# GpSimd in place of VectorE for the remainders of three norms' squares, with new step orders, in a two-layer hybrid decoder trunk

## The chip, the core and the metric

The kernel runs on one core of one Trainium2 chip. The metric is the time of one execution on the device, in microseconds (us). The kernel before was run three times: the median is 1242.65 us, the runs lie from 1242.56 to 1242.9 us.

Five engines work side by side, each on its own list of instructions in a fixed order: TensorE (PE in the profile, with PEld for its weight loads), VectorE (DVE), ScalarE (ACT), GpSimd (POOL) and SyncE (SP), which issues the transfers between the device's memory (HBM) and the on-chip buffer. An engine that meets a wait on a semaphore stands still until the semaphore has the value, and everything behind it in its list stands too.

## The reference

Two layers of a trunk for 528 tokens (16 learned meta tokens and 512 of the sequence), model width 1024. Cut to what matters:

```
a = rms_norm(h, attn_norm)
proj = a @ w_in                           # 24 units of 128 columns
dq, dk, iq, ik -> rms_norm (dq, dk only), partial_rope
o_a = dsa_attention(...)                  # index scores, top 128 keys, softmax over them
fq, fk -> rms_norm;  o_b = forgetting_attention(...)
o_c = gla_chunked(...);  o_c = rms_norm(o_c) * silu(gg)
h = h + concat(o_a, o_b, o_c) @ w_out
f = rms_norm(h, ffn_norm);  h = h + (silu(gate) * up) @ w_down
```

The norms of this case are the ones over heads of 64 (dk, dq, fq, fk) or 128 columns (o_c): x times the inverse root of the mean of its squares.

## The kernel before

**Data.** Features lie on the 128 partitions, tokens along the row. A weight unit is a 128x1024 tile. Every product of TensorE that must be exact is made of parts: ScalarE rounds a tile to a high part (`whi`, `xhi`), another engine subtracts it from the tile to get the low part (`wlo`, `xlo`), and TensorE sums high times high, high times low and low times high. So each weight unit of the projections needs a rounding on ScalarE (L1713) and a split on GpSimd (L891, four instructions of 128x256) before TensorE can do its low pass (L1136).

**The norm of a head unit k.** ScalarE squares the unit twice: in full into `sqb` (L1784) and rounded into `sq_parts[:, 1]` (L1785). One subtraction, the remainder, fills `sq_parts[:, 0]`. TensorE sums both parts over the head with a matrix of ones (`norm`, L1150, four matmuls). ScalarE makes the inverse root with a logarithm and an exponential (L1758, L1793), VectorE multiplies the unit by it (L2276). There is one `sqb` and one `sq_parts`, so ScalarE squares the next unit only after TensorE's sums of the one before. Eleven units are normed in each layer, in the order of NORM_ORDER: 0 (dk with ik), 4 and 5 (dq), 6 and 7 (fq), 8 and 9 (fk), and 16 to 19 (o_c). For the first three the remainder is on VectorE (`square_left`, L2285, semaphore `sq_left`), for the other eight on GpSimd (`square_parts`, L984, semaphore `sq_split`).

**From norm 0 to the index scores.** After norm 0, SyncE gathers the rotary rows of units 0, 1 and 2 into `xnb` (L826, three transfers), TensorE swaps them (`rope`, L1159), VectorE rotates them (L2303 to L2306), SyncE spreads them back (L836), ScalarE and VectorE split keys (`split_k`, L1798 and L2312, tile `kk`) and queries (`split_q`, L1809 and L2319), and TensorE makes the index products (`index`, L1204), which ScalarE reads (L1904) and VectorE sums.

**Order.** In the mixers (projections and attention, ahead of the feed-forward part) the order of the steps on each engine is a string of letters for each layer and engine (STEPS_OF, L261), one letter for each chain of steps; the chains are listed in L184. BANKS_OF (L285) gives the PSUM bank of each small job of TensorE. Of a projection half there are three pieces: two of high products (L1130, L1131) and one low pass (L1136). Behind the mixers everything is written out in the code.

Of the kernel before, what the change touches and what calls it, by code (L numbers as in the profile page):

```python
# [260 lines left out]
STEPS_OF = (  # L261
    {PE: "AAAAAAAAAAAABAAAAADAAAAAAFAAALAAAAAAAAAADAAAMMADAMMMMMMAMAAAMADAAAAPAAAADAAAAAAAAAPXXAAAAADXAXAAAAaL"
         "bAALAADAAAAAAAAXXXAXXdAXaXAYAYXXMMAAAbMAAMaAAdYZXAZXAYAXAYZZbXAAYAAAAZYYdXZZALXAAPARRAPLAYXZXYMAMaAb"
         "aALYdZAAYZXAXXAAYAZZbAYYZXXdZXZLYAAXYTSSZaRAATRbTARSSATTYAaAAdDXAZZYYXXXDZZbYAYAAdZDAYZAaAADZYAXXZbA"
         "XYAAXdAXYZaYXYZXZYXZbYYaZZYdZZfbfdfff",
     ACTE: "AABCDAAPIHLIACHADCIMMIDMMMMMMACMMDCIIAADCJOPAPIIPJDXAXXCXaALJLDAJAXXXXeaXXYYXMMMAXMaeYXXAYYPXXAKYYeX"
           "YLXPAPLXYYMXMaaYLAYeXXXXYYYeXLYYTaXAATTXXTTCYaUeCDXYYCXDYXAeYDXCYDYaUXXUYXXeAYaYUXXYYXXVYVVYVYAaee",
     DVEE: "AAACADAAAFAPIAAHIACHADCMMIIDMMMMMMAAFADANNNAADNINAINAXAIIANNXXOXDANANNNANNNDNANNNcXAXXXXPeXXAAXMMXMM"
           "NANNcAPPXXPNAXANcPeXAAXeNNXNNRRANNXMMAMXMAcNNNXNNeAXXANcNXXeNXNXASSRRNcNRSSNNANNAUeXNDXXNNcDXNAeADNN"
           "NNDXXUAXcXAAeXXUUXVVXcVWVWWWcee",  # L270
     POOLE: "QAAAQAAACACAACAACAQQAAAAQQAAAAACCCCAAA",
     DMAE: "AAEEEGAAAAEEGAAAAAAAAAAAAAAAAAA"},
    {PE: "AAAAAAAAABADAAAAAAFAAAAAALAMMDAAMADAMMMMAMMAAMADAAAADAAAAAAAAXXADAAAAYXAXYAMaMAMAADMAAAALLAAPXZZAYAP"
         "AAAAAYXXAAAXAAAAYYZZAAXbaAAYAAXAALZAYYZXZXAZAAAYXAMaAAAARARAALMAPPALbLASSTARATRSTdSRATYZZXYTAAYZYXZd"
         "XXbDAAYYZZadADXZZYXXbXXYAaZZYYXDAAdZZYYXbXYZXZZYaYXdZbXYZdXYZaXYZXYZXYbYDZZdYZaZbfdffff",
     ACTE: "BACADAAIIHACLIMMDHACMIDMMMMCMMAADCODMAIICADIIXXCXYYXMMAaMMADJJJPJLLAPPAXPYYXXAYYAXAaXLYYXYPXYXAMKaAL"
           "MPPXLALTTTAeTYYUTCXAYYXeDCXXYaeYUDYXXXYCaAYYUDXXXCeYYUYXXYaXeYYXeXVVaYAXYVXYXYXDYYVaee",
     DVEE: "AACDAAAFIIAAHCIMMDAHCMIDMMAMMFNAMDNAADIINXAAADXIIXXAMMMOMNNNNADNANPNANXNNNANNNNAPAXXANNNNXNNNAXPAXcA"
           "NPPAXXMNAPMNMXANARRNNMAANNNSNNSRNNRASNcRNSeNXNNNNXXecXADNNeUNXAXXDcXNNXXNNDNUAXcXXeUUVXecXVeXWVXXXcW"
           "DVWWcee",  # L280
     POOLE: "QQAAAAAACACAACACAAQQAAQAAAQAAAACCCAACA",
     DMAE: "AEEEAAGAAEEAGAAAAAAAAAAAAAAAAAA"},
)

BANKS_OF = (  # L285
    "0022023023012323220023103300030130213012013000232021011203210220202013200230321030210213013031030102"
    "0201203212002132030121203020203023013020320312",
    "0202012203203032000123210203102021030201231302300312030202020202031102010311303132031011203103013122"
    "0320132020220310130130101302301203",
)  # L290
# [2751 lines left out]
```

## Time and profile before

One profiled execution took 1242.44 us; its span, from the first to the last instruction, is 1240.7 us, so that 1.74 us lie around it. It is 0.21 us below the median of the three runs.

| what | before |
|---|---|
| median of 3 runs | 1242.65 us |
| profiled execution | 1242.44 us, span 1240.7 us |
| granted clock of TensorE | 1.0 over the span |
| TensorE busy | 1233.1 us, 99% of the span |
| VectorE, ScalarE, GpSimd busy | 83%, 57%, 16% |
| remainders on VectorE, on GpSimd | 6 and 16 |

The mixers of layer 0 lie between about 20 and 248 us of the span, those of layer 1 between about 647 and 865 us. A row of a timeline has the start, the time, the engine, the line of the kernel, what is written and read, and in brackets how long the engine was idle before it and what ended that. Matmuls are pipelined, so their times overlap; the distance from one start to the next tells how fast they go.

### The profile page before, as it was taken

The page shows a single profiled execution, that of the slowest core. Times are in us where ns is not written, and L with a number is a line of the kernel's source. Part 1 is how long each engine was busy: PE and PEld are TensorE (multiplying, and loading weights), DVE is VectorE, ACT ScalarE, POOL GpSimd, SP SyncE. Part 2 cuts the span into 40 slices and gives each one's busy share as a digit, 9 for nine tenths or more (in the row PEclk, how much of TensorE's full clock was granted, in tenths as well). Part 3 has the DMA queues.
Part 4 walks back from the last instruction along what each step waited for, and adds up shares of the span by engine and source line. Part 5 has one row for each costly group of instructions (what it writes and reads, how often), then busy time and mean ns, then how long its engine had stood idle before and what let it go on. Part 6 is the DMA issues. An engine that isn't in the chain of part 4 may idle for free.

```text
span 1240.7 us, 23938 instructions
## 1 busy us (share of the span) xinstructions
PE 1233.1 (99%) x9379; PEld 1185.1 (96%) x9379; DVE 1028.2 (83%) x1700; ACT 701.4 (57%) x1165; POOL 201.5 (16%) x264
## 2 busy tenths in 40 slices
PE   9999999999999999999999999999999999999999
PEld 9999999999999999999998999888889999998998
DVE  5788979588999999897666888985899999989765
ACT  6684547665555555753355765495665555558332
POOL 3565322100000000000035664230000000000000
PEclk9999999999999999999999999999999999999999
DMA  5222110132322221233323222110323322212333
GB/s 215 87 74 82 55 52 18 36 136 100 105 103 103 102 102 69 86 103 116 107 86 109 89 72 83 35 35 18 136 102 126 113 104 102 102 69 85 120 119 119
DMA packets 27244, 114.02 MB, mean 92 GB/s; under 512 B 3456, under 2 KB 3968, under 8 KB 21760
## 3 DMA queue, kind: packets, MB, share of 16 engines
q1 hardware_dynamic: 26704, 111.74, 26.6%
q8 instruction: 73, 1.20, 0.4%
q10 hardware_dynamic: 432, 0.80, 0.2%
q14 instruction: 35, 0.29, 0.1%
HBM read 108.79 MB, written 2.10 MB: 89 GB/s over the span
## 4 chain that ended last, share of the span: by engine, by line
PE 98%; ACT 1%; DVE 0%; issue 0%; POOL 0%; ACTq 0%; DVEq 0%
PE ps L1415 23%; PE ps L1421 11%; PE ps L1027 11%; PE ps L1130 7%; PE ps L1136 7%; PE ps L1131 7%; PE ps L1033 5%; PE ps L1499 5%; PE ps L1535 4%; PE ps L1256 3%; PE ps L1504 2%; PE ps L1540 2%; PE ps L1204 2%; PE ps L1229 2%; PE ps L1239 1%; PE ps L1150 1%
## 5 line engine op out<-in xcount | busy, mean ns | idle before, releaser
L891 POOL TENSOR_TENSOR wlo<-raw,whi 128x256 fp32r<-128x256 f32 x192 | 150.5, 816 | 144.7 <-ACT whi L1713 144.2
L1130 PE MATMUL ps<-xhi,whi 128*128 128x264 f32 (+1 forms) x616 | 172.1, 308 | 0.0
L1131 PE MATMUL ps<-xlo,whi 128*128 128x264 f32 (+1 forms) x616 | 167.3, 300 | 0.0
L1130 PEld LDWEIGHTS ps<-xhi,whi 128*128 128x128 f32 x616 | 116.1, 188 | 4.2 <-issue 0.4
L1131 PEld LDWEIGHTS ps<-xlo,whi 128*128 128x128 f32 x616 | 116.2, 189 | 3.4
L1713 ACT ACTIVATE whi<-raw 128x1024 fp32r<-128x1024 f32 x74 | 78.0, 1055 | 60.7 <-PE ps L1033 28.2
L1136 PE MATMUL ps<-xhi,wlo 128*128 128x264 f32 (+1 forms) x616 | 99.8, 304 | 0.0
L1136 PEld LDWEIGHTS ps<-xhi,wlo 128*128 128x128 f32 x616 | 85.2, 188 | 4.0
L1415 PE MATMUL ps<-fhi,hi_a 128*128 128x264 f32 (+1 forms) x352 | 88.2, 283 | 0.0
L1415 PE MATMUL ps<-flo,hi_a 128*128 128x264 f32 (+1 forms) x352 | 88.1, 282 | 0.0
L1415 PE MATMUL ps<-fhi,hi_b 128*128 128x264 f32 (+1 forms) x320 | 80.3, 283 | 1.8 <-ACT s L2037 1.8
L1415 PE MATMUL ps<-flo,hi_b 128*128 128x264 f32 (+1 forms) x320 | 80.3, 283 | 0.0
L2037 ACT ACTIVATE w_part<-ps 128x264 f32<-128x264 f32 (+1 forms) x42 | 16.3, 388 | 97.4 <-PE ps L1421 97.4
L923 POOL MEMSET lr_parts<- 80x532 f32 x2 | 1.1, 544 | 414.8 <-DVE wlo L2756 400.6
L2148 ACT ACTIVATE whi<-raw 128x1024 fp32r<-128x1024 f32 (+2 forms) x42 | 38.3, 913 | 50.4 <-PE ps L1504 30.4
L1415 PE MATMUL ps<-xlo,hi_a 128*128 128x264 f32 (+1 forms) x264 | 66.5, 283 | 0.0
L1415 PE MATMUL ps<-xhi,hi_a 128*128 128x264 f32 (+1 forms) x264 | 66.3, 283 | 0.0
L1415 PEld LDWEIGHTS ps<-flo,hi_a 128*128 128x128 f32 x352 | 66.3, 188 | 0.0
L1415 PEld LDWEIGHTS ps<-fhi,hi_a 128*128 128x128 f32 x352 | 66.2, 188 | 0.0
L1415 PEld LDWEIGHTS ps<-fhi,hi_b 128*128 128x128 f32 x320 | 60.3, 188 | 2.1 <-ACT hi_a L1996 2.1
L1415 PEld LDWEIGHTS ps<-flo,hi_b 128*128 128x128 f32 x320 | 60.3, 188 | 0.0
L1415 PE MATMUL ps<-xlo,hi_b 128*128 128x264 f32 (+1 forms) x240 | 59.9, 282 | 0.0
(377 smaller groups left out, 3885.1 us busy)
## 6 DMA issues: line engine op xcount, KB each, us to landing
raw<-in_weights SPq DMA_DIRECT2D x115, 512.0 KB, 3.5
raw<-in_groups SPq DMA_DIRECT2D x42, 1024.0 KB, 4.8
h<-in_hT SPq DMA_DIRECT2D x7, 264.0 KB, 6.4
out_hT<-h SPq DMA_DIRECT2D x7, 256.0 KB, 4.6
cst<-in_consts SPq DMA_DIRECT2D x1, 908.5 KB, 8.7
xnb<-feat SPq DMA_DIRECT2D x10, 66.5 KB, 2.1
feat<-xnb SPq DMA_DIRECT2D x10, 66.5 KB, 2.1
cst<-in_consts SPq DMA_DIRECT2D x1, 532.0 KB, 3.5
```

The lines of the kernel that those rows point to most:

```text
L891: ins = nc.gpsimd.tensor_tensor(wlo[:, b, of], raw[:, b, of], whi[:, b, of].bitcast(F32), ALU.subtract)
L1027: nc.tensor.matmul(bank(bank_no, cut.stop - cut.start), whi[:, b, k % KT], x(k)[t][:, cut], start=(first and k == ks[0] and t == 0), stop= ...
L1033: ins = nc.tensor.matmul(bank(bank_no, cut.stop - cut.start), wlo[:, b, k % KT], x(k)[0][:, cut], start=False, stop=(last and k == ks[-1]))
L1130: nc.tensor.matmul(o, whi[:, k % 2, n], xhi[:, n, cut], start=(n == 0), stop=False)
L1131: nc.tensor.matmul(o, whi[:, k % 2, n], xlo[:, n, cut], start=False, stop=False)
L1136: ins = nc.tensor.matmul(o, wlo[:, k % 2, n], xhi[:, n, cut], start=False, stop=(n == KT - 1))
L1415: nc.tensor.matmul(bank(bank_no, width), high[:, of], x(i)[t], start=(begins and i == 0 and t == 0), stop=False, skip_group_check=True)
L1421: ins = nc.tensor.matmul(bank(bank_no, width), low, x, start=False, stop=(n == PAIRS - 1), skip_group_check=True)
L1499: nc.tensor.matmul(to, whi[:, slot, k], hidden_tiles(k0 + k)[t][:, cut], start=(begins and k == 0 and t == 0), stop=False, skip_group_chec ...
L1535: nc.tensor.matmul(down_bank(l, bank_no), high(i), x(i)[t], start=(begins and i == 0 and t == 0), stop=False, skip_group_check=True)
L1713: return nc.scalar.activation(whi[:, b], raw[:, b], ACT.Copy).then_inc(hi_done, 1)
L2148: nc.scalar.activation(whi[:, slot, 0:tiles], raw[:, slot, 0:tiles], ACT.Copy).then_inc(hi_done, 1)
```

## The change

The remainders of units 0, 4 and 5 go to GpSimd as well: the two kinds of step become one (`square`), the semaphore `sq_left` goes, and TensorE waits for `sq_split` alone. The strings of STEPS_OF and BANKS_OF are replaced as a whole, for both layers and all engines.

```diff
-LEFT_TO_VECTOR = (DKIK, DQ, DQ + 1)
-LEFT_TO_GPSIMD = (FQ, FQ + 1, FK, FK + 1, GV, GV + 1, GV + 2, GV + 3)
...
-def square_step(k):
-    return ("square_left" if k in LEFT_TO_VECTOR else "square_parts", k)
...
-        "square": [square_step(k) for k in NORM_ORDER],
+        "square": [("square", k) for k in NORM_ORDER],
...
-     POOLE: "QAAAQAAACACAACAACAQQAAAAQQAAAAACCCCAAA",
+     POOLE: "QAACQAAACACCAACAACAACQQAAAAQQAAAAACCCCAAA",
...
-    "prenorm": (PE, ACTE), "square_left": (ACTE, DVEE), "square_parts": (ACTE, POOLE), "norm": (PE, ACTE, DVEE),
+    "prenorm": (PE, ACTE), "square": (ACTE, POOLE), "norm": (PE, ACTE, DVEE),
...
-        self.sq_left = sem(f"sq_left_of{l}")
...
-                    if k in LEFT_TO_VECTOR:
-                        pe.wait_ge(ev.sq_left, LEFT_TO_VECTOR.index(k) + 1)
-                    else:
-                        pe.wait_ge(ev.sq_split, LEFT_TO_GPSIMD.index(k) + 1)
+                    pe.wait_ge(ev.sq_split, SQUARES[k] + 1)
...
-                def square(k):
-                    dve.wait_ge(ev.sq_ready, 2 * SQUARES[k] + 2)
-                    nc.vector.tensor_tensor(sq_parts[:, 0], sqb[:, 0], sq_parts[:, 1].bitcast(F32), ALU.subtract).then_inc(ev.sq_left, 1)
```

Three places show what the new strings move. The lines of the changed kernel have other numbers (the remainder is L976 there, the weight split L883, the sums of a norm L1139, the low pass L1128, the rounding of a unit L1702).

TensorE, layer 0, around the sums of norm 0; before:

```order
L1131 MATMUL ps<-xlo,whi 128x264
L1130 MATMUL ps<-xhi,whi 128x264
L1131 MATMUL ps<-xlo,whi 128x264
L1150 MATMUL ps<-sq_parts,ones_r 128x266 x4
L1136 MATMUL ps<-xhi,wlo 128x264 x8
L1130 MATMUL ps<-xhi,whi 128x264
```

and changed:

```order
L1123 MATMUL ps<-xlo,whi 128x264
L1122 MATMUL ps<-xhi,whi 128x264
L1123 MATMUL ps<-xlo,whi 128x264
L1128 MATMUL ps<-xhi,wlo 128x264 x8
L1139 MATMUL ps<-sq_parts,ones_r 128x266 x4
L1122 MATMUL ps<-xhi,whi 128x264
```

The sums of norm 0 stand one low pass later. The `rope` products stand as many projection pieces from the start as before, so that one piece less lies between the two.

GpSimd, layer 1, from the clearing of `q_odd` to the weight splits; before:

```order
L946 MEMSET k_fox 64x2x532 x2
L947 MEMSET q_odd 64x1064
L910 COPY q_odd<-cst 4x532 x2
L891 TENSOR_TENSOR wlo<-raw,whi 128x256 x24
L984 TENSOR_TENSOR sq_parts<-sqb,sq_parts 128x532
```

and changed:

```order
L938 MEMSET k_fox 64x2x532 x2
L939 MEMSET q_odd 64x1064
L902 COPY q_odd<-cst 4x532 x2
L976 TENSOR_TENSOR sq_parts<-sqb,sq_parts 128x532
L883 TENSOR_TENSOR wlo<-raw,whi 128x256 x16
L976 TENSOR_TENSOR sq_parts<-sqb,sq_parts 128x532
L883 TENSOR_TENSOR wlo<-raw,whi 128x256 x4
```

The remainder of unit 0 stands ahead of every weight split of the layer, and that of unit 4 ahead of the fifth.

ScalarE, layer 0, from the first query part to the rounding behind the squares of unit 4; before:

```order
L1809 ACTIVATE q_split<-feat 64x528
L1798 ACTIVATE kk<-feat 64x528 x2
L1818 ACTIVATE v_dsa<-ps 128x4x64
L1820 ACTIVATE v_meta<-ps 16x64 x4
L1821 ACTIVATE w_idx<-ps 128x20
L1809 ACTIVATE q_split<-feat 64x528
L1713 ACTIVATE whi<-raw 128x1024
L1784 ACTIVATE sqb<-feat 128x532
L1785 ACTIVATE sq_parts<-feat 128x532
L1798 ACTIVATE kk<-feat 64x528 x2
L1713 ACTIVATE whi<-raw 128x1024
```

and changed:

```order
L1798 ACTIVATE q_split<-feat 64x528 x2
L1787 ACTIVATE kk<-feat 64x528 x2
L1702 ACTIVATE whi<-raw 128x1024
L1807 ACTIVATE v_dsa<-ps 128x4x64
L1809 ACTIVATE v_meta<-ps 16x64 x4
L1810 ACTIVATE w_idx<-ps 128x20
L1787 ACTIVATE kk<-feat 64x528 x2
L1773 ACTIVATE sqb<-feat 128x532
L1774 ACTIVATE sq_parts<-feat 128x532
L1702 ACTIVATE whi<-raw 128x1024
```

The second half of the key split (`kk`) now stands ahead of the squares of unit 4.

## Rows read from the trace of the kernel before

**Rows 1.** The page: busy time by engine; chain that ended last, by engine.
```profile
PE 1233.1 (99%) x9379; PEld 1185.1 (96%) x9379; DVE 1028.2 (83%) x1700; ACT 701.4 (57%) x1165; POOL 201.5 (16%) x264
...
PE 98%; ACT 1%; DVE 0%; issue 0%; POOL 0%; ACTq 0%; DVEq 0%
```
**Rows 2.** Waits of TensorE, whole span: who for whom, us, times, longest.
```profile
PE ps L1415 <- ACT s L2037: 1.8, 2, 0.9
PE ps L1004 <- DVE kk L2216: 1.2, 1, 1.2
PE ps L1204 <- ACT relu L1904: 0.5, 1, 0.5
PE ps L1204 <- DVE q_keys L2319: 0.3, 1, 0.3
PE ps L1192 <- issue: 0.2, 1, 0.2
PE ps L1150 <- POOL sq_parts L984: 0.2, 1, 0.2
PE ps L1204 <- DVE mix_hi L2319: 0.2, 1, 0.2
```
**Rows 3.** The remainders by source line: ns min/median/max, first and last start.
```profile
L984 POOL TENSOR_TENSOR sq_parts<-sqb,sq_parts x16: 1320/1339/1807, 60.4 to 829.6; 128x532 fp32r<-128x532 f32 x16
...
L2285 DVE TENSOR_TENSOR sq_parts<-sqb,sq_parts x6: 711/868/1139, 25.2 to 675.2; 128x532 fp32r<-128x532 f32 x6
```
**Rows 4.** Timeline of GpSimd, then ScalarE, layer 0, 19 to 26 us.
```profile
19.73 5.60 POOL L891 TENSOR_TENSOR wlo<-raw,whi 128x256 fp32r<-128x256 f32 x8 [1.01 <-ACT whi L1713]
...
24.53 0.64 ACT L1785 ACTIVATE sq_parts<-feat 128x532 fp32r<-128x532 f32 x1
```
**Rows 5.** TensorE from norm 0: chain of waits (start, us, what), then timeline.
```profile
26.78 0.98 PE ps L1136 x8
...
32.51 1.11 PE L1159 MATMUL ps<-xnb,cst 96*96 96x266 f32 x4
```
**Rows 6.** SyncE's gather before `rope`: timeline, then `xnb` transfers' landing times.
```profile
29.03 1.82 SPq L826 DMA_DIRECT2D xnb<-feat  x3
...
DMA to landing us min/median/max: 1.9/2.1/3.4
```
**Rows 7.** Timeline of ScalarE, layer 0, the squares of units 4 and 5.
```profile
44.52 0.63 ACT L1785 ACTIVATE sq_parts<-feat 128x532 fp32r<-128x532 f32 x1
45.06 1.29 ACT L1798 ACTIVATE kk<-feat 64x528 fp32r<-64x528 f32 x2
...
47.82 0.69 ACT L1758 ACTIVATE rnb<-ps,cst 128x532 f32<-128x532 f32 x1
...
49.63 0.63 ACT L1785 ACTIVATE sq_parts<-feat 128x532 fp32r<-128x532 f32 x1
```
**Rows 8.** Timeline of TensorE, layer 0, norms 4, 5, 6 and three index waits.
```profile
46.65 0.65 PE L1150 MATMUL ps<-sq_parts,ones_r 128*128 128x266 f32 x4
...
51.67 0.74 PE L1150 MATMUL ps<-sq_parts,ones_r 128*128 128x266 f32 x4
...
53.58 0.42 PE L1204 MATMUL ps<-kk,mix_hi 128*128 128x144 f32 x2 [0.19 <-DVE mix_hi L2319]
54.32 0.42 PE L1204 MATMUL ps<-kk,q_keys 128*128 128x144 f32 x2 [0.32 <-DVE q_keys L2319]
...
57.21 0.64 PE L1204 MATMUL ps<-kk,q_split 128*128 128x400 f32 x2 [0.45 <-ACT relu L1904]
...
61.95 0.68 PE L1150 MATMUL ps<-sq_parts,ones_r 128*128 128x266 f32 x4
```
**Rows 9.** Timeline of ScalarE, layer 0, the squares of unit 6.
```profile
59.69 0.64 ACT L1785 ACTIVATE sq_parts<-feat 128x532 fp32r<-128x532 f32 x1
...
61.16 0.50 ACT L1904 ACTIVATE relu<-ps 128x400 f32<-128x400 f32 x1 [0.44 <-PE ps L1204]
```
**Rows 10.** Timeline of layer 1's start: GpSimd, then TensorE.
```profile
645.95 1.30 POOL L910 COPY q_odd<-cst 4x532 f32<-4x532 f32 x2
647.33 3.22 POOL L891 TENSOR_TENSOR wlo<-raw,whi 128x256 fp32r<-128x256 f32 x4
...
648.50 0.66 PE L1150 MATMUL ps<-sq_parts,ones_r 128*128 128x266 f32 x4
...
650.83 2.02 PE L1136 MATMUL ps<-xhi,wlo 128*128 128x512 f32 x8
```
**Rows 11.** Weight splits of GpSimd, ns min/median/max: whole span, then 44 to 53 us.
```profile
L891 POOL TENSOR_TENSOR wlo<-raw,whi x192: 720/738/1773, 19.7 to 845.6; 128x256 fp32r<-128x256 f32 x192
...
L891 POOL TENSOR_TENSOR wlo<-raw,whi x8: 734/1147/1216, 44.2 to 50.9; 128x256 fp32r<-128x256 f32 x8
```

More of the change, by code:

```diff
@@ L261 @@
 STEPS_OF = (
[L262 to L270, printed above, removed]
-     POOLE: "QAAAQAAACACAACAACAQQAAAAQQAAAAACCCCAAA",
-     DMAE: "AAEEEGAAAAEEGAAAAAAAAAAAAAAAAAA"},
@@ L273 @@
[L273 to L282, printed above, removed]
+    {PE: "AAAAAAAAAAAABAAAAAADAAAAAFAAAAAALAAAAAAAADAAMMADAMMMMAMMAMMAAADAPAAAAAAAAAAADAXXAAAAAPAXAAADAAAXAALA"
+         "AALAAADaAAbAAAAXXAAXXXdXAXaAbXYAMMYAXAMAAMAadXZYYAAZAZZbYAXXXAAAYAAZdYAAYXXAAZALPARRAZPLAXYYXZMAMaAA"
+         "AbaAZdZLYAYXXZZYbAAXXYAAYZdAXXYZLXZYTSSRAaAATRZTbRSSATTYAZadAAZDXXAYYXAYDZZXbAAYDZAdAAAYYZDaAZAAXZbX"
+         "XAYXAAdYXZaXYYZXYZXZbYYaZZYdZZbfdffff",
+     ACTE: "AABCDAAPIIHALHCAIDCIMMDMMMMMMMMCADIAPCIOADIICAXPAJXPDCAXXLJLAaJDJXXXAXXaeYXXMMXYAMMaYXYYXXAPYXAeYeKX"
+           "XYALPXPLYYMMXaaXeLYYAXXYAXXeYYYLYXTXaTXTTATYCeaUDCXXYYDYCAXXDCeYYYaUDUXXYXXeYAXaYUXYXYXVYVVaYYVAee",
+     DVEE: "AAAADAAFAAAPIIAHHAADMMIIDMMMMMMAAFNADANANIIAADANXNNXIINAAXONNNDXAAANNNPANNDNNNXXNcXAAXXXAXXMeMMMXNNc"
+           "APNPAXAPXXNcNAAXPeeAXXNNNARRNNXMNMMXMAAcNNNeXXNNNXXcAAeXXNXNSSRNNNRcRSSNNNAAeNNXDXXANDUXcNNDAeNNAANN"
+           "DXUXXXceXUAAXXUVXVcVVWWWWcee",
+     POOLE: "QAACQAAACACCAACAACAACQQAAAAQQAAAAACCCCAAA",
+     DMAE: "AAEEEGAAAEEGAAAAAAAAAAAAAAAAAAA"},
@@ new lines @@
+    {PE: "AAAAAAAAABADAAAAAAFAAAAAALMMADAAMADAMMMAMAAAMMDMAAAAADAAAAAADXAAXYAAAXXAAMMYAAMAAaADAMZZALAAALAXYPAA"
+         "AAYPYAXAXZAAAXZbYAAAYXAAAZaAAXAAAZZLAAYYXAXZYAAAAMAXAAaRRAAALMAPPAALLASTASRATRbSTdSRZZAYTYXZZTYXbYXA"
+         "dXDAZAdaYYZAZZXDAXXbYAXYYXZZaAYDXAZZYYXbdXYZXZaYZYXZdbXYZdXYZaXZYXYZXYbYDZYdaZZZbffdfff",
+     ACTE: "BACDAAAIIHAICLMMDHCMAIDMMAMMCAMDCJOAIDCIMMADXIIPXCXYMMMYXAaAJJDJLMALXYPAYPPXXXYAAAaYYLXXYYYPXXMKAaLM"
+           "PPAXLLTTATUeYAYTXTCYYeCXDXYaeAYUDXCYXXXYUXYaYDXXAYYUXYXeaYAYXeXYeXCYaXVVYYXXYXDYaVYVee",
+     DVEE: "AADAAFAAIIAHIMMDAHMIDMMAMMFAMDNNAADIIAAXDIXIAXXMNMMMAPOAANNNDNNNNANNXNNNNNAANNXXNAAXNNNNcAAXPPAXNNAP"
+           "PXXMMPMXNAARRANNNMNAANNNSNNSRNNRSAcSReUNNXNNNXXNcXeNADNNeXNNXXDAcNXXNNXDANUUXcXUXVeVVXceXeXXXXcWWDVW"
+           "Wcee",
+     POOLE: "QQCAAAACACAACACCAACAAQQQAAAAAQAAAACCCACAA",
+     DMAE: "AEEEAAGAAEAEGAAAAAAAAAAAAAAAAAA"},
@@ L283 @@
 )
 BANKS_OF = (
[L286 to L289, printed above, removed]
+    "0022023023012323220230013000330130210301302100230211201220312020202102300232031032021031031031031002"
+    "0201203212010233020211302020203203103020320312",
+    "0202012203203030202013212301002020312030121230300312003202020202013102010313130130213013012010133201"
@@ L290 @@
+    "2302320120202310130130101302302103",
 )
 ON = {
-    "prenorm": (PE, ACTE), "square_left": (ACTE, DVEE), "square_parts": (ACTE, POOLE), "norm": (PE, ACTE, DVEE),
+    "prenorm": (PE, ACTE), "square": (ACTE, POOLE), "norm": (PE, ACTE, DVEE),
     "gather": (DMAE,), "rope": (PE, DVEE), "spread": (DMAE,), "split_k": (ACTE, DVEE),
@@ L985, in square @@
                     halved[0] += 1
-                do = dict(proj=proj, square_parts=square, masks=masks, clear_fox=clear_fox, spread_sums=spread_sums, clear_even=clear_even,
+                do = dict(proj=proj, square=square, masks=masks, clear_fox=clear_fox, spread_sums=spread_sums, clear_even=clear_even,
                           clear_gla_even=clear_gla_even, clear_gla_odd=clear_gla_odd)
@@ L1969, in gla_mix @@
                     nc.scalar.activation(mix_hi[:, 4 + hd], feat[:, place(GG + hd)], ACT.Copy).then_inc(ev.gla_hi, 1)
-                do = dict(prenorm=prenorm, proj=proj, square_left=square, square_parts=square, norm=norm, split_k=split_k, split_q=split_q_hi, part=part, even_q=even_q,
+                do = dict(prenorm=prenorm, proj=proj, square=square, norm=norm, split_k=split_k, split_q=split_q_hi, part=part, even_q=even_q,
                           turn_tile=turn_tile,
@@ L2532, in gla_lo @@
                                             ALU.subtract).then_inc(ev.gla_split, 1)
-                do = dict(proj=proj, square_left=square, norm=norm, rope=rope, split_k=split_k, split_q=split_q_lo, gate_split=gate_split, gate_log=gate_log, gate_sum=gate_sum, gate_arg=gate_arg,
+                do = dict(proj=proj, norm=norm, rope=rope, split_k=split_k, split_q=split_q_lo, gate_split=gate_split, gate_log=gate_log, gate_sum=gate_sum, gate_arg=gate_arg,
                           fox_log=fox_log, decays=decays, index=index, topk=topk, lowest=lowest,
```

## The prediction

> **What bounds the kernel.** Three views were read. First the busy times and the chain that ended last: TensorE is busy for 1233.1 us of a span of 1240.7, and the chain is 98% TensorE [rows 1]. The change takes no instruction from TensorE and adds none; its matmuls come in another order. So what counts is where TensorE stands still. The second view, its waits over the whole span, says how little that is: seven kinds, 4.4 us together, of which the two waits of 1.8 and 1.2 us lie outside the mixers. That leaves 1.4 us in the mixers, five kinds of 0.2 to 0.5 us [rows 2], and only there do the new strings reach. Of the engines that the change touches, only 0.2 of it waits for GpSimd and none for a remainder on VectorE: its line L2285 is not among those waited for [rows 2]. The third view, timelines around the moved steps, tells how much time each had to spare.
>
> So the removal as such is worth next to nothing, and the question is what GpSimd and the new orders make late.
>
> **What the removal frees.** Six remainders (three units, two layers) leave VectorE: six times a median of 0.87 is 5.2 us [rows 3], at 83% busy [rows 1]. TensorE waits for VectorE in the mixers for 0.3 + 0.2 us [rows 2]. These are the most that a freer VectorE can give.
>
> **What it adds.** Six remainders of the same 128x532 on GpSimd, at a median of 1.34 us there (1.32 to 1.81) [rows 3]. GpSimd is busy for 16% [rows 1], so 8 us more are nothing as a total. What costs is the place: a remainder stands in GpSimd's list between weight splits, waits there for ScalarE's squares, and TensorE's sums wait for it; 1.34 against 0.87 also lengthens each of the six chains by about 0.5 us.
>
> **Layer 0, norm 0 and the rope.** GpSimd's first eight splits end at 19.73 + 5.60 = 25.33, the squares at 24.53 + 0.64 = 25.17 [rows 4], so the remainder runs from 25.33 to 26.67. TensorE has norm 0 one low pass later; the low pass that now comes ahead of it takes 0.98 and began at 26.78 behind norm 0 [rows 5]. With 0.65 for four sums of a norm [rows 8], norm 0 began at about 26.1 and will at about 27.1: later than 26.67, no wait. But the rope keeps its place in the count of projection pieces, at 32.51 [rows 5], and its chain starts 0.98 later. Before, the three gathers end at 29.03 + 1.82 = 30.85; the third is issued at about 30.3 and lands 2.1 later by the median, at 32.4 [rows 6]. The rope had 0.1 us to spare or a little more, and now lacks 0.8 to 1.0. I take +0.9.
>
> **Norm 4.** On ScalarE the second pair of key halves goes ahead of the squares: the time to square is 45.15, when the squares of unit 4 end now (44.52 + 0.63), so two squares of 0.63 or a little more reach 45.15 + 1.29 = 46.4 if the pair is only put ahead, and up to 47.3 if they are also released 0.9 later by the late rope [rows 7]. The remainder ends at 47.8 to 48.7, with 1.81 for it at 49.2. TensorE had norm 4 at 46.65 [rows 8]; it comes one piece later (0.97, as the low pass of [rows 5]) and 0.9 of the rope's wait later, at 48.5. Between nothing and 0.7; I take +0.4, near the later squares, since keys wait for the rope as well.
>
> **Norm 5.** It needs norm 4 first, as there is one `sq_parts`. From the logarithm of norm 4 (47.82) to the end of the squares of unit 5 (49.63 + 0.63) ScalarE takes 2.44 [rows 7]. Norm 4 at 48.9 and its 0.65 [rows 8] make 49.6; plus 2.44 is 52.0, plus 1.34 is 53.4, at worst 53.8. TensorE's place for norm 5 is 51.67 [rows 8] plus the 1.3 lost so far, 53.0. I take +0.6 of 0.4 to 0.9.
>
> **Index and norm 6.** Behind two such waits the index products come later than their parts, and the three small waits of 0.19, 0.32 and 0.45 [rows 8] go: −1.0. The squares of unit 6, which end at 60.3, now stand behind the two relus of 400 keys, the first of which begins at 61.16 [rows 9]; norm 6 was at 61.95 [rows 8]. Two relus of 0.50, two squares of 0.64 and 1.34 would reach past it by more than 1 us if TensorE had not itself moved back by 1 to 2 us and a piece. Between 0 and 1.4; I take +0.4, nearer to none, as TensorE's delay is the nearest row. Layer 0: 0.9 + 0.4 + 0.6 − 1.0 + 0.4 = +1.3.
>
> **Layer 1, the first weight unit.** GpSimd's list now has the remainder of unit 0 ahead of all splits. It is free at 645.95 + 1.30 = 647.25; the remainder takes the place of the split at 647.33 and ends at 648.67. Norm 0 stood at 648.50: +0.2. The first unit's four splits took 3.22, to 650.55, and the low pass that needs them started at 650.83 [rows 10], 0.28 behind. Now they end at 651.9, or at 651.6 if each takes the median of 0.74 [rows 11]: the low pass is late by 0.8 to 1.1 in all. I take +1.0, the 0.2 of norm 0 in it. Queued behind these splits are all later ones, but those had units of lead to spare.
>
> **The rest of layer 1.** One block of index products stands ahead of a projection piece that it used to follow, so its key parts may be late: 0 to 0.6, taken as +0.2. The wait of 0.2 for `sq_parts` of GpSimd and the 0.2 of no seen releaser [rows 2] belong to a norm and a gate that now come one piece later: −0.4. Layer 1: +0.8. Other moved steps are costed at nothing, because TensorE stands for 0 us at their like in the list of waits [rows 2]; with that cover gone each costs its chain's excess, a few tenths.
>
> **Sum.** +1.3 + 0.8 = +2.1 on the profiled execution of 1242.44 (span 1240.7 and 1.74 around it) is 1244.5 us. The median of the runs is 0.21 higher, which I leave in the range.
>
> **A rule that speaks for more.** Between 44 and 53 us the eight splits took a median of 1.15 us against 0.74 over the whole span, so GpSimd is slowed there by something [rows 11]. The Trainium skill, "SBUF — State Buffer", section "Who interferes with whom", says that a VectorE instruction with two inputs in that buffer contends with a GpSimd instruction that reads it, and that whichever issues first holds the shared ports for the whole instruction. By that rule a remainder can cost 1.34 plus a VectorE operation of 0.7, about 2.05 (an estimate with that page's rule), against the longest seen, 1.81; the trace agrees in kind, and the sum would be 1247 instead of 1244.5 if all six were hit, which is in the second case's upper part.
>
> **The rivals.** *GpSimd's queue becomes the bound (slower).* A remainder that waits for squares holds every split behind it, and those hold low passes. Six remainders at 1.81 instead of 1.34 are +2.8 at most if all lie on the path, and norm 6 at its end of 1.4 is +1.0 more than taken. For it: the splits at 1.15 us where norms 4 and 5 lie [rows 11], and the 0.28 us of spare at the first low pass of layer 1 [rows 10]. Against it: GpSimd's 16%, and that a wait at one step covers the next. About half of these, +1.8 on my sum, is 1246.3; up to 1248. It decides from new waits of 3.9 us, which less the 1.4 of old ones pass 2.5 us.
>
> *Nothing new waits.* The late parts are covered because TensorE's order gives each norm a piece more, and only old waits go, or the new cost equals them: −1.4 to +0.5, 1241.0 to 1243.0, with 1241.9 as its time. For it: norms 0 and 4 do stand a piece later. Against it: the rope does not, and its slack of 0.1 is in the rows [rows 5, 6]; the first split of layer 1 is delayed by a whole remainder and no row shows time for it [rows 10].
>
> *Faster by more than the measure.* What can be told from no change is about 0.2%, 2.5 us, here below 1240.2. All mixer waits of TensorE are 1.4 [rows 2], so this needs matmuls that themselves go faster in the new order. No row shows such.
>
> **How the numbers follow.** Forecast 0.48, with its own range of 1243.2 to 1245.1; queue as the bound 0.35; nothing new 0.12; faster 0.05. The first and third lie within 2.5 us of 1242.65: same 0.60. Slower 0.35, faster 0.05. The range from 1242.3 (half of the third case left out) to 1247.2 (the tail of the second left out) leaves about 2 in 10.
>
> **What would show it.** In the waits of TensorE after: at the rope, for the `xnb` transfers, about 0.9; at the norms for `sq_parts` of GpSimd, 1 to 1.6 together; at the low pass of layer 1, for `wlo` of GpSimd, about 0.8 to 1; and the three index waits gone. The 4.4 us of waits become about 6.5. VectorE's busy time falls by 5 us and GpSimd's rises by 8. I am wrong if the waits in the mixers sum to less than 1.4 us, if they pass 5, or if the span moves and they do not; in the last case the order itself would change how fast matmuls follow each other.

## The result: slower by 4.8 us, above the forecast range

The changed kernel takes 1247.43 us in the median (1246.87 to 1247.91, 6 runs) against 1242.61 (6 runs) for the kernel before: a ratio of 1.0038, with a 95% interval of 1.0028 to 1.0048. The forecast was 1244.5, its range 1242.3 to 1247.2: the sign was right, the size less than half of what was measured. The profiled execution took 1246.87 us, 0.56 below the median, with a span of 1245.1.

The page of the changed kernel, busy times by engine and the chain that ended last [rows 1]:

```profile
PE 1234.4 (99%) x9379; PEld 1185.2 (95%) x9379; DVE 1021.6 (82%) x1694; ACT 702.6 (56%) x1165; POOL 206.6 (17%) x270
...
PE 93%; POOL 2%; DVE 2%; ACT 2%; issue 1%; DMA 1%; SPq 0%; ACTq 0%; DVEq 0%; POOLq 0%
```

VectorE is freed of 6.6 us and GpSimd has 5.1 more, where 5 and 8 were forecast; GpSimd's remainders add 7.9, its weight splits take 3.2 less. The chain now leaves TensorE for 7% of the span instead of 2%: it runs mostly through GpSimd, VectorE and ScalarE. The waits of TensorE (engine, tile and line, then whom for: us, times, longest) [rows 2]:

```profile
PE ps L1139 <- POOL sq_parts L976: 2.4, 4, 0.9
PE ps L1404 <- ACT s L2026: 1.8, 2, 0.9
PE ps L996 <- DVE kk L2205: 1.2, 1, 1.2
PE ps L1148 <- DMA xnb<-feat: 0.8, 1, 0.8
PE ps L1128 <- POOL wlo L883: 0.6, 2, 0.4
```

All five small waits of the mixers are gone and 3.8 us of new ones have come, 3.0 of them for GpSimd. So the list holds 6.8 us where it held 4.4, and shows only 2.4 of the 4.4 us by which the span grew. The rest stands in no listed wait: TensorE's idle time (span less busy time) grew by 3.1 us in all, short gaps included, and its busy time by 1.3. The new waits in TensorE's timeline (start, us, line, operation; in brackets the idle time and its end):

```profile
33.68 0.44 PE L1148 MATMUL ps<-xnb,cst 96*96 96x266 f32 x1 [0.78 <-DMA xnb<-feat]
...
54.04 0.36 PE L1139 MATMUL ps<-sq_parts,ones_r 128*128 128x266 f32 x1 [0.89 <-POOL sq_parts L976]
...
63.97 0.36 PE L1139 MATMUL ps<-sq_parts,ones_r 128*128 128x266 f32 x1 [0.60 <-POOL sq_parts L976]
...
75.05 0.39 PE L1128 MATMUL ps<-xhi,wlo 128*128 128x264 f32 x1 [0.20 <-POOL wlo L883]
...
680.05 0.36 PE L1139 MATMUL ps<-sq_parts,ones_r 128*128 128x266 f32 x1 [0.32 <-POOL sq_parts L976]
...
703.82 0.36 PE L1139 MATMUL ps<-sq_parts,ones_r 128*128 128x266 f32 x1 [0.61 <-POOL sq_parts L976]
707.48 0.39 PE L1128 MATMUL ps<-xhi,wlo 128*128 128x264 f32 x1 [0.44 <-POOL wlo L883]
```

These are the rope, norms 5 and 6 and the low pass of unit 9 in layer 0, then norms 5 and 8 and the low pass of unit 10 in layer 1. Units 6 and 8 had their remainder on GpSimd before as well, and with the new orders alone (below) their norms still wait, 0.49 and 0.31 us; so these waits come at least in part from the order of the lists.

To see what each layer lost, three marks were read in every trace: the first projection product of layer 0's mixers, and the first product of the feed-forward part of each layer. Before:

```profile
20.94 0.48 PE L1130 MATMUL ps<-xhi,whi 128*128 128x264 f32 x1
...
294.93 0.28 PE L1415 MATMUL ps<-xhi,hi_a 128*128 128x264 f32 x1
...
909.81 0.28 PE L1415 MATMUL ps<-xhi,hi_a 128*128 128x256 f32 x1
```

and after the change:

```profile
21.14 0.48 PE L1122 MATMUL ps<-xhi,whi 128*128 128x264 f32 x1
...
297.47 0.28 PE L1404 MATMUL ps<-xhi,hi_a 128*128 128x264 f32 x1
...
914.22 0.28 PE L1404 MATMUL ps<-xhi,hi_a 128*128 128x256 f32 x1
```

From mark to mark layer 0 costs 2.34 us more (276.33 against 273.99) and layer 1 costs 1.87 more; from the last mark to the end the traces differ by 0.01. The first mark varies by up to 0.5 us from the kernel before's although nothing ahead of it was changed; the marks leave that part out. They come from one execution of each kernel, and executions of one kernel differ by up to 2.2 us (1243.54 to 1245.74 for orders_norm0_back), so single tenths of them prove nothing.

### The profile page after: what moved, and what is told of

Its sections match the earlier page's. It is cut to its first block, busy times and chain, and to the rows that moved or that the text cites. A ratio compares the mean times of both kernels' runs of the same rounds, so it can differ in the third digit from the quotient of the medians.

```text
span 1245.1 us, 23934 instructions
## 1 busy us (share of the span) xinstructions
PE 1234.4 (99%) x9379; PEld 1185.2 (95%) x9379; DVE 1021.6 (82%) x1694; ACT 702.6 (56%) x1165; POOL 206.6 (17%) x270
## 4 chain that ended last, share of the span: by engine, by line
PE 93%; POOL 2%; DVE 2%; ACT 2%; issue 1%; DMA 1%; SPq 0%; ACTq 0%; DVEq 0%; POOLq 0%
PE ps L1404 23%; PE ps L1410 11%; PE ps L1019 10%; PE ps L1128 6%; PE ps L1122 6%; PE ps L1123 5%; PE ps L1025 5%; PE ps L1524 4%; PE ps L1488 4%; PE ps L1245 3%; PE ps L1529 2%; PE ps L1493 2%; PE ps L1218 2%; PE ps L1193 1%; PE ps L1228 1%; POOL wlo L883 1%
## 5 line engine op out<-in xcount | busy, mean ns | idle before, releaser
L883 POOL TENSOR_TENSOR wlo<-raw,whi 128x256 fp32r<-128x256 f32 x192 | 147.3, 799 | 146.7 <-ACT whi L1702 146.3
L1702 ACT ACTIVATE whi<-raw 128x1024 fp32r<-128x1024 f32 x74 | 78.1, 1055 | 59.4 <-PE ps L1025 29.9
L1128 PE MATMUL ps<-xhi,wlo 128*128 128x264 f32 (+1 forms) x616 | 100.2, 305 | 0.7 <-POOL wlo L883 0.6
L1128 PEld LDWEIGHTS ps<-xhi,wlo 128*128 128x128 f32 x616 | 84.6, 188 | 5.5 <-POOL wlo L883 1.6
L1404 PE MATMUL ps<-xhi,hi_b 128*128 128x264 f32 (+1 forms) x240 | 59.9, 282 | 0.0
```

The source lines that it names most:

```text
L883: ins = nc.gpsimd.tensor_tensor(wlo[:, b, of], raw[:, b, of], whi[:, b, of].bitcast(F32), ALU.subtract)
L1128: ins = nc.tensor.matmul(o, wlo[:, k % 2, n], xhi[:, n, cut], start=False, stop=(n == KT - 1))
L1404: nc.tensor.matmul(bank(bank_no, width), high[:, of], x(i)[t], start=(begins and i == 0 and t == 0), stop=False, skip_group_check=True)
L1702: return nc.scalar.activation(whi[:, b], raw[:, b], ACT.Copy).then_inc(hi_done, 1)
```

## The experiments

At first there were two theories. O: the new orders cost the time (rope, norms 6 and 8 wait although their remainders did not move). Q: the remainder on GpSimd costs it, longer by 0.5 us and in a queue with the weight splits. Times are medians; "before" is the kernel before in the same comparison; the last two columns are the differences from mark to mark against the trace before.

| kernel | us | before | ratio (95%) | layer 0 | layer 1 |
|---|---|---|---|---|---|
| changed | 1247.43 | 1242.61 | 1.0038 (1.0028 to 1.0048) | +2.34 | +1.87 |
| engine_alone | 1246.68 | 1242.9 | 1.0032 (1.0020 to 1.0044) | +2.83 | +1.36 |
| orders_alone | 1245.9 | 1242.9 | 1.0023 (1.0014 to 1.0032) | +2.92 | +0.49 |
| double_remainders | 1254.76 | 1242.9 | 1.0097 (1.0081 to 1.0112) | +6.21 | +5.48 |
| mended | 1247.57 | 1242.9 | 1.0038 (1.0025 to 1.0052) | +3.32 | +1.76 |
| unit0_moved | 1243.97 | 1242.52 | 1.0013 (1.0004 to 1.0022) | +0.64 | +0.85 |
| unit4_moved | 1244.92 | 1242.52 | 1.0018 (1.0009 to 1.0027) | +1.56 | +0.96 |
| unit5_moved | 1244.48 | 1242.52 | 1.0016 (1.0007 to 1.0025) | +1.07 | +0.49 |
| before_mended | 1242.98 | 1242.52 | 1.0004 (0.9995 to 1.0013) | +0.01 | −0.05 |
| unit5_held | 1246.9 | 1242.4 | 1.0034 (1.0021 to 1.0048) | +3.03 | +1.33 |
| before_held | 1245.53 | 1242.4 | 1.0025 (1.0015 to 1.0034) | +2.64 | +0.62 |
| orders_norm0_back | 1244.82 | 1242.47 | 1.0018 (1.0009 to 1.0027) | +1.08 | +0.33 |
| after_norm0_back | 1247.07 | 1242.47 | 1.0036 (1.0022 to 1.0050) | +2.60 | +2.17 |

**The engine alone.** The changed code with all lists of before; only GpSimd's got the six remainders, as the squares come ready.

```diff
-     POOLE: "QAAAQAAACACAACAACAQQ...        (layer 0)
+     POOLE: "QAACAQACACACACAACAACAQQ...
-     POOLE: "QQAAAAAACACAACACAAQQ...        (layer 1)
+     POOLE: "QQCAAAACACACACAACACAAQQ...
```

> The six remainders on GpSimd, all other orders as before (GpSimd's own list takes each where its squares are ready). Theory O (the new orders cost most of the 4.8 us): at most +1.8 us over before, worked out as 0.6 at norm 0 of layer 0 (remainder 25.33 to 26.67 against TensorE at 26.07), 0.6 at the start of layer 1, 0.4 at norm 5 of layer 1: 1243.0 to 1244.4. Theory Q (the remainder on GpSimd, longer and in a queue, costs most): +3 or more, 1245.6 and up, with waits of TensorE for sq_parts of GpSimd at norms 4 and 5.

**The orders alone.** The new lists of the change, with the three remainders back in VectorE's list and out of GpSimd's.

```diff
-     DVEE: "AAAADAAFAAAPIIAHHAADMMIID...     (layer 0)
+     DVEE: "AAACADAAFAAAPIIAHHACADCMMIID...
-     DVEE: "AADAAFAAIIAHIMMDAHMID...         (layer 1)
+     DVEE: "AACDAAFAAIIAHICMMDAHCMID...
```

> The orders of the changed kernel, the six remainders back on VectorE. Theory O: the wait at the rope (0.8), those at norm 6 of layer 0 and norm 8 of layer 1 (0.6 each, both of units whose remainder was always on GpSimd) and at a low pass (0.4) stay: 1245.3 to 1247. Theory Q: these go with the queue, at most +1.5 us over before, up to 1244.1.

Measured: +3.8 us for the engine alone, +3.0 for the orders alone, +4.8 for both. Neither theory holds by itself: each half alone costs more than the theory that lays the loss on the other half allows (+1.8 and +1.5). The marks separate them by layer. In layer 1 the halves add up (1.36 and 0.49 against 1.87), and the engine is nearly three quarters of it. In layer 0 they do not (2.83 and 2.92 against 2.34): there the orders take back part of what the engine costs, and the engine part of the orders'. With the lists of before, the split of unit 6 and the remainder of unit 4 meet in GpSimd's list; this is its timeline in the kernel with the engine alone, and what TensorE then waits for:

```profile
46.22 1.34 POOL L976 TENSOR_TENSOR sq_parts<-sqb,sq_parts 128x532 fp32r<-128x532 f32 x1 [4.99 <-ACT sq_parts L1774]
47.51 4.22 POOL L883 TENSOR_TENSOR wlo<-raw,whi 128x256 fp32r<-128x256 f32 x4
```

```profile
51.78 0.39 PE L1128 MATMUL ps<-xhi,wlo 128*128 128x264 f32 x1 [1.41 <-POOL wlo L883]
```

GpSimd stands for 4.99 us in front of a remainder whose squares are not made yet, and behind it the split, which began at 44.2 in the kernel before [rows 11], starts at 47.51. With the remainder on VectorE the two ran side by side. The changed kernel puts the split first and norm 4 one piece later, and has no 1.41 there.

**Twice the remainder.** The changed kernel with a second instruction behind each of the six.

```diff
+ if SQUARES[k] < 3:
+     nc.gpsimd.tensor_tensor(sq_parts[:, 0], sqb[:, 0], ..., ALU.subtract).then_inc(ev.sq_first, 1)
+     pool.wait_ge(ev.sq_first, SQUARES[k] + 1)
+     nc.gpsimd.tensor_tensor(sq_parts[:, 0], ..., ALU.add).then_inc(ev.sq_split, 1)      (sq_parts[:, 0] added to itself)
```

> The changed kernel with a second GpSimd instruction of 128x532 behind each of the six remainders (it adds the low part to itself, so the low part of these squares is doubled). Each extra takes about 1.4 us. Theory Q: norms 4 and 5 of both layers and the first low pass of layer 1 stand directly behind the remainder, +1.4 at five of six places: +5 to +7 over the changed kernel, about 1253. Theory O: the orders have room at most places, +1 to +4: 1248.4 to 1251.4, and less than 1.4 per place.

The second instruction and who waited for it, by source line:

```profile
L980 POOL TENSOR_TENSOR sq_parts<-sq_parts x6: 1071/1072/1176, 27.0 to 686.4; 128x532 fp32r<-128x532 f32 x6
...
  PE ps L1145: 8.2, 6
```

Six times 1.07 is 6.4 us; the kernel became 7.0 us slower (11.86 over the kernel before, against 4.82 for the changed kernel). TensorE waited for all six. So next to nothing covers a longer remainder in these places (in the changed kernel the sums begin 0.47 us behind it at norm 0 of layer 0, 0.14 to 0.20 us at the other five), and theory Q has this much right: on GpSimd, each sits on the path. No run doubles a remainder on VectorE.

**One unit at a time.** The lists of before, with one unit's remainder moved to GpSimd in both layers. Here the theories are P (the price depends on what stands beside it) and E (each costs alike).

```diff
-LEFT_TO_VECTOR = (DKIK, DQ, DQ + 1)
+LEFT_TO_VECTOR = (DKIK, DQ)                 (for unit 5; the others likewise)
-     POOLE: "QAAAQAAACACA...                 (layer 0)
+     POOLE: "QAACAQAAACACA...  (unit 0)   "QAAAQACAACACA...  (unit 4)   "QAAAQAACACACA...  (unit 5)
```

> The kernel before with only unit 0's remainder on GpSimd (both layers), all other orders as before. Theory P (a remainder costs by what stands beside it in GpSimd's list): norm 0 of layer 0 +0.6, start of layer 1 +0.6, so +1.2 us over before. Theory E (any remainder on GpSimd costs alike, a third of the +3.8 that all three units cost): +1.3. This run tells them apart only with the next two.

> The kernel before with only unit 4's remainder on GpSimd, placed ahead of the split of unit 6. Theory P: in layer 0 the split waits for the squares at 45.15 and its low pass comes late by 1.4 to 1.6, nothing in layer 1: +1.5 us over before. Theory E: +1.3, in both layers alike.

> The kernel before with only unit 5's remainder on GpSimd, placed ahead of the split of unit 7, which has 8 us to spare in layer 0. Theory P: nothing in layer 0, 0.4 to 0.6 at norm 5 of layer 1: +0.3 to +0.8 us over before. Theory E: +1.3.

Measured: +1.45, +2.4 and +1.96 us. The intervals reach about 1.1 us to either side, so the times alone do not tell the units apart and do not exclude E; nor do they tell whether such prices add up (the three make 5.8 us, all three at once cost 3.8 with the engine alone). By the marks P is right on unit 0 (0.64 and 0.85), on unit 4 in layer 0 (1.56) and on unit 5 in layer 1 (0.49). It is wrong at two places: unit 4 in layer 1 (0.96 where nothing was expected) and unit 5 in layer 0 (1.07 where nothing was). Both have the same main cause. With unit 5 moved, TensorE in layer 0 waits like this:

```profile
54.31 0.42 PE L1204 MATMUL ps<-kk,mix_hi 128*128 128x144 f32 x2 [0.29 <-DVE mix_hi L2319]
55.47 0.42 PE L1204 MATMUL ps<-kk,q_keys 128*128 128x144 f32 x2 [0.74 <-DVE q_keys L2319]
...
58.72 0.45 PE L1204 MATMUL ps<-kk,q_split 128*128 128x400 f32 x1 [0.81 <-ACT relu L1904]
```

It waits for VectorE, which has one instruction less to do. The two instructions by source line, before and with unit 5 moved (ns min/median/max):

```profile
L2319 DVE TENSOR_TENSOR mix_hi<-feat,mix_hi x1: 702/702/702, 52.7 to 52.7; 64x528 fp32r<-64x528 f32 x1
L2319 DVE TENSOR_TENSOR q_keys<-feat,q_keys x1: 704/704/704, 53.5 to 53.5; 64x528 fp32r<-64x528 f32 x1
```

```profile
L2319 DVE TENSOR_TENSOR mix_hi<-feat,mix_hi x1: 1121/1121/1121, 53.0 to 53.0; 64x528 fp32r<-64x528 f32 x1
L2319 DVE TENSOR_TENSOR q_keys<-feat,q_keys x1: 1127/1127/1127, 54.2 to 54.2; 64x528 fp32r<-64x528 f32 x1
```

and GpSimd at the same time, with unit 5 moved:

```profile
50.82 1.34 POOL L984 TENSOR_TENSOR sq_parts<-sqb,sq_parts 128x532 fp32r<-128x532 f32 x1 [2.41 <-ACT sq_parts L1785]
52.11 3.80 POOL L891 TENSOR_TENSOR wlo<-raw,whi 128x256 fp32r<-128x256 f32 x4
```

The split of unit 7 ended at 52.1 before the move. Behind the remainder it runs until 55.9, beside VectorE's key and query parts, and both slow down: VectorE's from 0.70 to 1.12, the splits to 0.95 each. In layer 1, unit 4's move does the same to VectorE's remainder of unit 5 (1.13 instead of 0.76) and to the scaling and the key parts ahead of it, and norm 5 waits 0.86 for it. The Trainium skill, "SBUF — State Buffer", section "Who interferes with whom", has the rule (a VectorE instruction with two inputs in that buffer and a GpSimd instruction that reads it contend); the traces agree, with 0.70 against 1.12.

**Holding the split away.** To test this (theory C: the split beside VectorE's chain costs the time; D: the longer remainder does), the split of unit 7 waits until VectorE has scaled unit 5, in both layers, once with unit 5 moved, once in the kernel before.

```diff
  def proj(k, hf, p):
+     if k == 5:
+         pool.wait_ge(ev.normed, 3)
```

> The kernel with only unit 5's remainder on GpSimd, and GpSimd's split of unit 7 held until VectorE has scaled unit 5 (it waits for that semaphore; its low pass has over 1 us to spare after that). With the remainder ahead of it, that split lay beside VectorE's mix_hi, q_keys and scaling, which took 1.12 to 1.13 us instead of 0.70 to 0.77. Theory C (the moved split slows VectorE's chain of two-input instructions): they take 0.70 to 0.78 again, the 1.1 us lost in layer 0 shrink to 0.2 to 0.4, time 1243.4 to 1243.8. Theory D (the longer remainder alone delays the chain): layer 0 keeps its 1.1 us, time 1244.2 to 1244.8.

> The kernel before with the same hold on the split of unit 7, all remainders on VectorE. Theory C: VectorE's scaling of unit 4 and the remainder of unit 5, at 1.15 and 1.12 us beside that split, take 0.7 to 0.9; the index products' waits of 0.19 and 0.32 shrink or go: 0.2 to 0.6 us less than before. Theory D: as before within 0.2.

Both times are far outside what either theory expected, +4.5 and +3.1 us. The part that was to be tested came out as C says: with unit 5 moved and the split held, VectorE takes

```profile
L2321 DVE TENSOR_TENSOR mix_hi<-feat,mix_hi x1: 702/702/702, 51.9 to 51.9; 64x528 fp32r<-64x528 f32 x1
L2321 DVE TENSOR_TENSOR q_keys<-feat,q_keys x1: 705/705/705, 52.6 to 52.6; 64x528 fp32r<-64x528 f32 x1
```

and the index waits of 0.29 and 0.74 shrink to less than 0.1. TensorE gains by it up to there. These are the first mark and the `q_keys` products in the kernel before with the split held:

```profile
20.55 0.48 PE L1132 MATMUL ps<-xhi,whi 128*128 128x264 f32 x1
...
53.03 0.42 PE L1206 MATMUL ps<-kk,q_keys 128*128 128x144 f32 x2
```

They lie 32.48 us apart, against 33.38 in the kernel before [rows 8], 0.9 less; with unit 5 moved the hold gains 1.2 (32.86 against 34.06).

But the split has to be somewhere: now it lies beside the sums of the scores, which also read two tiles. Two of 128x144 take 1.70 there instead of 0.77 with unit 5 moved and the split not held. ScalarE waits for these sums to free its `relu` buffers, TensorE for ScalarE, 2.5 us in one piece. This is VectorE with unit 5 moved, not held:

```profile
56.52 0.77 DVE L2400 SCALAR_TENSOR_TENSOR score<-relu,w_idx,score 128x144 f32<-128x144 f32 x2
```

This is VectorE, unit 5 moved and held:

```profile
54.55 1.70 DVE L2402 SCALAR_TENSOR_TENSOR score<-relu,w_idx,score 128x144 f32<-128x144 f32 x2
56.28 0.71 DVE L2407 SCALAR_TENSOR_TENSOR score<-score,causal 128x144 f32<-128x144 f32 x1
```

and these are ScalarE, in the second of its two waits for VectorE, and TensorE:

```profile
57.97 0.94 ACT L1906 ACTIVATE relu<-ps 128x272 f32<-128x272 f32 x2 [1.23 <-DVE score L2398]
...
58.42 0.79 PE L1206 MATMUL ps<-kk,q_split 128*128 128x400 f32 x2 [2.52 <-ACT relu L1906]
```

So the slowing that C speaks of is shown, in both directions; the shorter time that it forecast is not. The same 3 us of GpSimd's work cost TensorE 0.9 us where they lay in the kernel before (beside the scaling of unit 4 and the remainder of unit 5), 1.2 beside the key and query parts, and a wait of 2.5 us in place of 0.45 beside the sums. In the kernel before with the hold, a gain of 0.9, this longer wait (+2.0), the slower clock behind it (+1.3, last section) and 0.6 in layer 1 make 3.0 of the 3.1 us.

**Pieces moved ahead of what waits.** In the changed kernel, and then in the kernel before.

```diff
  mended (layer 0, TensorE): a piece ahead of the rope and of norm 4, two ahead of norms 5 and 6
-  ...AAAAADAAAAAFA...   ...DAAMMADAMMMMAMMAMMAAADAPA...
+  ...AAAAADAAAAAAF...   ...ADAMMAAADMMMMMMAMMAAAAADP...
  before_mended (layer 0, TensorE):
-  ...DAMMMMMMAMAAA...
+  ...DAAMMMMMMAMAA...
```

> The changed kernel with projection pieces moved ahead of the steps that wait in its trace: one ahead of the rope, one ahead of norm 4, two ahead of norm 5, two ahead of norm 6 in layer 0; one ahead of norms 5 and 8 in layer 1, and GpSimd's split of unit 10 ahead of the remainder of unit 8 there. The remainders stay on GpSimd. Theory O: the waits of 0.78, 0.89, 0.60 and of 0.32, 0.61, 0.44 go, 2.5 to 3.6 us less: 1243.8 to 1245. Theory Q: the waits only move to the next step, at most 1 us less: 1246.4 and up.

> The kernel before with one projection piece moved ahead of the index products that wait 0.19 and 0.32, one ahead of those that wait 0.45 (layer 0), and one ahead of norm 7 of layer 1 (0.20). If TensorE waits there for want of a piece in front: 0.7 to 1.1 us less than before. If the wait moves on to the next product of the same chain, as in the changed kernel with pieces moved: within 0.4 us of before, with new waits behind the old places.

Mended, the changed kernel loses its norm waits but for 0.2 us and takes the same time: 1247.57 against 1247.43. TensorE waits one step further on:

```profile
55.73 0.31 PE L1193 MATMUL ps<-kk,mix_hi 128*128 128x144 f32 x1 [0.50 <-DVE mix_hi L2304]
56.47 0.31 PE L1193 MATMUL ps<-kk,q_keys 128*128 128x144 f32 x1 [0.32 <-DVE q_keys L2304]
59.76 0.45 PE L1193 MATMUL ps<-kk,q_split 128*128 128x400 f32 x1 [0.86 <-ACT relu L1893]
67.13 0.39 PE L1181 MATMUL ps<-lr_parts,w_parts 80*128 80x266 f32 x1 [0.85 <-ACT rnb L1747]
```

The kernel before does it too: its 0.19 and 0.32 go, and norm 6, which had no wait, gets 0.73 (for `sq_parts` of GpSimd, at 61.80). In layer 1 the wait of 0.20 at norm 7 goes, and norm 8, which had none, gets 0.41 (at 701.62). The sum is zero. So in these stretches the chain over ScalarE, VectorE and GpSimd is about as long as TensorE's work, and a wait that is pushed off comes back further down.

**Norm 0 one piece earlier.** As it stood before, once with VectorE's remainders and once with GpSimd's.

```diff
-    {PE: "AAAAAAAAAAAABAAAAAADAAAAAF...
+    {PE: "AAAAAAAAAAAABAAAAADAAAAAAF...
```

> The new orders with VectorE's remainders, and norm 0 of layer 0 one projection piece earlier, where it stood in the kernel before. VectorE's remainder is done there before TensorE comes, so nothing waits at norm 0 and the rope's wait of 0.77 goes. If that wait is a loss of its own: 0.6 to 1.0 us less than with the new orders alone, 1244.9 to 1245.3. If what it gave back is waited for again at norms 4, 5 and 6, which hang on the same chain of keys: under 0.4 us less, 1245.5 and up.

> The changed kernel with norm 0 of layer 0 one piece earlier. GpSimd's remainder ends at 26.82 there and TensorE comes at 26.3: a new wait of about 0.5 for it, and the rope's 0.78 falls to 0.3 or less. If both are losses of their own: 0 to 0.4 us less than the changed kernel, 1247.0 to 1247.4; if the chain behind the rope takes it up, the same within 0.2, or up to 0.5 more.

With VectorE's remainder the rope's wait goes, and the loss falls from 3.0 to 2.35 us over the kernel before; the interval (1.0009 to 1.0027) overlaps that of the orders alone, so the size is open. Layer 0's marks fall from 2.92 to 1.08, but its profiled execution was its fastest (1243.54). With GpSimd's remainder the gain against the changed kernel is 0.2 us by the two differences to the kernel before, which is less than can be told, since the wait at norm 0 takes its place:

```profile
26.64 0.36 PE L1139 MATMUL ps<-sq_parts,ones_r 128*128 128x266 f32 x1 [0.55 <-POOL sq_parts L976]
...
49.06 0.36 PE L1139 MATMUL ps<-sq_parts,ones_r 128*128 128x266 f32 x1 [0.64 <-POOL sq_parts L976]
```

The rope has no wait here, norm 4 gets 0.64 where the changed kernel had none listed (its remainder took 1.90 us here, see below). With GpSimd's remainder, which ends later, either place of norm 0 costs about the same; with VectorE's the old place is the better one. No version was faster than the kernel before.

## Why the prediction was right or wrong

Measured is the difference of each step's start to the next step's start in the two traces.

| term | predicted | measured |
|---|---|---|
| rope | +0.9 | +0.9 |
| norm 4 | +0.4 | +0.2 |
| norm 5 | +0.6 | +0.9 |
| three index waits | −1.0 | −1.3 |
| norm 6 | +0.4 | +0.7 |
| all else in layer 0 | 0 | +0.9 |
| first unit of layer 1 | +1.0 | +0.6 |
| index block of layer 1 | +0.2 | +0.2 |
| two old waits of layer 1 | −0.4 | −0.7 |
| all else in layer 1 | 0 | +1.8 |
| ahead of the mixers | 0 | +0.2 |
| sum on the profiled execution | +2.1 | +4.4 |

**What was right.** No run shows a gain from VectorE's freed time, and the waits at the rope (0.78 for 0.9), norm 5 and norm 6 stand where they were put. The index waits went, as said. The list of waits came out as forecast in its sum, 6.8 us for 6.5, though not in its parts (2.4 for the remainders where 1 to 1.6 were said, nothing listed at the first low pass of layer 1); but it does not hold all that was lost. The first unit of layer 1 was taken too dear: its four splits took 2.83 us in place of 3.22 [rows 10].

**What failed** is one step: "Other moved steps are costed at nothing, because TensorE stands for 0 us at their like in the list of waits [rows 2]; with that cover gone each costs its chain's excess, a few tenths." The end of the sentence names the loss, but the sum has it at 0. These steps cost 2.7 us, more than the whole gap of 2.3. In layer 1 these are norm 8 with 0.77, the low pass of unit 10 behind it with 0.70, norm 5 with 0.39 and norm 6 with 0.29, less 0.4 elsewhere; in layer 0 the low pass of unit 9 with 0.5 and, for the rest, small changes around the steps that moved. A list of waits says where nothing was lost, not how much there was to spare. Norm 8 of layer 1 is not on the list of the kernel before, and these are its remainder and its sums there:

```profile
700.28 1.33 POOL L984 TENSOR_TENSOR sq_parts<-sqb,sq_parts 128x532 fp32r<-128x532 f32 x1
...
701.75 0.36 PE L1150 MATMUL ps<-sq_parts,ones_r 128*128 128x266 f32 x1
```

The sums begin 0.14 us behind the remainder's end, as close as at norm 7, which is on the list (691.71 and 691.85): there was nothing to spare, and the new order puts norm 8 two projection pieces earlier. VectorE's own remainders were misread in the same way: none is on the list, but the sums of norm 5 begin 0.15 us behind theirs in both layers, so 0.5 us more had no cover there. Norm 6 of layer 1, as little on the list, had 3.1 us. The runs show what stood in the place of nothing: a remainder's added time in full on the path (7.0 us for six extra instructions), and a chain from norm to norm that gave back the waits that were pushed off.

**The rivals.** The price of "GpSimd's queue becomes the bound", 1246.3 to 1248, holds the result; it had a chance of 0.35, the forecast 0.48. The engine's side is the greater part in layer 1 (engine alone 1.36 of 1.87), while in layer 0 orders and engine each cost as much, so its mechanism is not all of it. The argument that spoke against it, that a wait at one step covers the next, fails at the doubled remainders: the six added instructions cost all of their time. "Nothing new waits" and "faster" did not occur.

**The rule that spoke for more.** From the Trainium skill's rule the prediction took a longer remainder on GpSimd, up to 2.05 us, and a time of 1247. That time does not follow from its terms: six times 0.71 are 4.3, and 1244.5 with it is 1248.8. So it is luck that 1247 lies near the measured time. In the changed kernel the 22 remainders take 1.32 to 1.57, and it is VectorE that pays: a key part (`kk`) that begins together with the remainder of unit 4 took 1.88 us, its like 0.70. By source line, all remainders and then the key parts from 43 to 58 us (ns min/median/max):

```profile
L976 POOL TENSOR_TENSOR sq_parts<-sqb,sq_parts x22: 1315/1334/1574, 25.5 to 846.2; 128x532 fp32r<-128x532 f32 x22
...
L2297 DVE TENSOR_TENSOR kk<-feat,kk x4: 704/970/1883, 42.9 to 47.6; 64x528 fp32r<-64x528 f32 x4
```

With norm 0 one piece earlier (after_norm0_back) the same two begin together again, and it is the remainder that pays:

```profile
47.02 1.90 POOL L976 TENSOR_TENSOR sq_parts<-sqb,sq_parts 128x532 fp32r<-128x532 f32 x1 [0.58 <-ACT sq_parts L1774]
...
47.02 0.70 DVE L2297 TENSOR_TENSOR kk<-feat,kk 64x528 fp32r<-64x528 f32 x1
```

The weight splits of this stretch were quicker than before (a median of 0.74 for 1.15 [rows 11]), so that here the contention moved rather than grew. That it costs time is shown by the held split, and read from the waits for units 4 and 5 moved alone; its share of the changed kernel's 4.8 us stays open.

**The last 0.2 us.** By the profiled execution, 1246.87, the time would lie inside the range; the other runs lie up to 1.0 higher, so that the median passes its end.

## What to carry to other kernels

An engine that is busy for 16% is no free engine: what counts is what stands behind the moved instruction in its list and which instructions of its neighbour it then runs beside, so lay out the new list against the timeline of both. Where a list of waits shows nothing, work out the slack (ready time against start) for each moved step before costing it at zero. A wait that can be pushed off without a gain, as here twice, points to a chain as long as the work that hides it.
